# Two scatter accumulators, passes over low parts last, and merged operand splits in the experts of a decoder layer

## The reference, cut to what matters

```
scores = sigmoid(xt @ w_router)                 # 1024 tokens, 64 experts, group-limited top 8
top_w  = top_s / sum(top_s) * 2.5
# per expert e, for the tokens that chose it, in padded blocks:
hb = silu(xb @ w1[e]) * (xb @ w3[e])            # xb (block, 1024), w1 and w3 (1024, 256)
yb = hb @ w2[e]                                 # w2 (256, 1024)
routed = zeros.at[row_tok].add(yb * row_w)      # scatter-add
x = x + g2 * rmsnorm(routed + shared, norm_post_ffn)
```

## Time and profile before

| what | value |
| --- | --- |
| device time, median of 3 runs | 1926.11 us (1922.32 to 1934.88) |
| span of the profiled execution, first to last instruction | 1924.1 us |
| its device time as a whole | not recorded beside the span |
| mean granted TensorE clock | 0.957 |
| attention | about 350 to 498 us of the span |
| experts' loop, from its first to its last block | 941.4 to 1896 us |
| last stage, from the load of `acc` on | 1896.4 to 1924.1 us |

### The profile page before, as it was taken

How to read it: one execution, slowest core, us unless ns; L and a number is a source line. 1 busy time by engine, 2 the same in 40 slices (tenths; PEclk the granted TensorE clock), 3 DMA queues, 4 the chain that set the end, 5 groups by cost and what they waited for, 6 DMA issues and landing times. The chain is left out here.

```text
span 1924.1 us, 38146 instructions
## 1 busy us (share of the span) xinstructions
PE 1746.1 (91%) x10357; PEld 1353.5 (70%) x10358; DVE 1410.6 (73%) x2642; ACT 1137.8 (59%) x2188; POOL 465.8 (24%) x361
## 2 busy tenths in 40 slices
PE   3998999777599978998699999999999999999994
PEld 2787887555378756776577777777777677777773
DVE  6587651588478756666488888888888788888887
ACT  4411221477466543343477777777777677777776
POOL 0011100000022201336233333332333223333231
PEclk8999999999699978999799999999999999999997
DMA  9267610300200162428789978899888999899975
GB/s 358 82 197 208 199 53 28 130 16 17 93 6 8 33 232 77 111 79 173 243 266 294 298 220 277 252 311 332 266 260 292 315 302 284 259 285 300 316 233 194
DMA packets 132525, 380.04 MB, mean 198 GB/s; under 512 B 27365, under 2 KB 39998, under 8 KB 130380
## 3 DMA queue, kind: packets, MB, share of 16 engines
q1 hardware_dynamic: 97276, 288.36, 43.0%
q0 software_dynamic: 35168, 90.60, 19.5%
HBM read 333.82 MB, written 82.13 MB: 216 GB/s over the span
## 5 line engine op out<-in xcount | busy, mean ns | idle before, releaser
L2470 DVE TENSOR_TENSOR w_low<-w_experts,w_high 128x1024 fp32r<-128x1024 f32 x388 | 457.1, 1219 | 91.6 <-issue 63.4
L2411 ACT CAST w_high<-w_experts 128x1024 fp32r x390 | 390.0, 1049 | 94.8 <-issue 80.4
L2393 POOL DMA_INDIRECT acc<-y_rows,scatter_idx x96 | 185.0, 1927 | 604.8 <-DMA acc<-y_rows,scatter_idx 363.6
L2546 PE MATMUL rbank<-w_high,xT_high 128*128 128x512 f32 x776 | 314.7, 406 | 8.5 <-DVE xT_low L2485 8.5
L2546 PE MATMUL rbank<-w_high,xT_low 128*128 128x512 f32 x776 | 308.4, 397 | 0.0
L2546 PE MATMUL rbank<-w_low,xT_high 128*128 128x512 f32 x776 | 305.6, 394 | 0.0
L2568 PE MATMUL rbank<-w_experts,upper 128*128 x384 | 180.8, 593 | 1.9 <-DVE actT_low L2476 1.9
L2546 PEld LDWEIGHTS rbank<-w_high,xT_high 128*128 128x128 f32 x776 | 147.6, 190 | 40.2 <-DVE xT_low L2485 8.1
L2546 PEld LDWEIGHTS rbank<-w_high,xT_low 128*128 128x128 f32 x776 | 146.8, 189 | 33.4
L2546 PEld LDWEIGHTS rbank<-w_low,xT_high 128*128 128x128 f32 x776 | 147.4, 190 | 31.0
L2377 POOL DMA_INDIRECT gathered<-h,idx x96 | 137.5, 1432 | 44.5 <-issue 27.1
(11 more groups left out here) (445 smaller groups left out, 3611.7 us busy)
## 6 DMA issues: line engine op xcount, KB each, us to landing
w_experts<-in_exp_w SPq DMA_DIRECT2D x384, 512.0 KB
qT<-in_w_ada POOLq DMA_DIRECT2D x16, 1024.0 KB, 6.0
w_raw<-in_w_in SPq DMA_DIRECT2D x24, 512.0 KB, 6.8
w_ada<-in_w_ada SPq DMA_DIRECT2D x16, 512.0 KB, 15.1
p_mixed<-mixed SPq DMA_DIRECT2D x8, 512.0 KB, 8.4
w_out<-in_w_out SPq DMA_DIRECT2D x1, 4096.0 KB, 12.5
x_kept<-x SPq DMA_DIRECT2D x8, 512.0 KB
acc_tile<-acc SPq DMA_DIRECT2D x8, 512.0 KB, 7.1
```

What stands on the lines that cost most here:

```text
L2393: pool.indirect_dma_start(dr["acc"], bass.IndirectOffsetOnAxis(ap=sidx[j][:], axis=0), y[j % 2][:], None, bounds_check=S - 1, oob_is_err=F ...
L2411: act.copy(w13_s[par][0][:, which, k], w13[:, bass.ds(w, 1), which, k].squeeze(1)).then_inc(w_high, 1)
L2470: dve.tensor_tensor(w13_s[par][1][:, which, k], w13[:, bass.ds(w, 1), which, k].squeeze(1), w13_s[par][0][:, which, k], ALU.subtract).then ...
L2546: q = pe.matmul(ps_h[:].rearrange("p (a n) -> p a n", a=2), xT[a][:, k, :], w13_s[par][z][:, :, k, :], start=(k == 0 and m == 0), stop=(k ...
```

## The change

- `attend`: VectorE clears a tile of 128x1024 first of all, and SyncE writes it eight times to `acc1`, a second accumulator in HBM (4 MB), between the eight loads and the stores of `o`.
- `experts`: blocks with an even number scatter to `acc`, those with an odd number to `acc1`, each with a semaphore of its own, so that a scatter waits for the one two before it. In the end both are loaded, and VectorE adds them tile by tile.
- The copy of block `b`'s result out of PSUM moves on ScalarE from the end of turn `b` into turn `b + 1`, behind the high part of `w2`.
- Pairs of instructions become one: the two copies of `y_rows`, the two high parts and two low parts of the transposed rows, the pairs of weight splits (2048 elements instead of two times 1024; 1024 instead of two times 512 for `w2`), and the two index columns (one tile of two columns; the scatter reads its first, the gather its second).
- The copy of the gate weight (`slot_w`) moves from VectorE to ScalarE.
- TensorE does the passes over low parts last: in `up` all eight slices high-high, then all with the low part of the weights, then all with the low part of the rows, with a wait ahead of each pass; in `down` the native half first, then high-high and low-high, then the pass with the low part of `w2`.
- VectorE's turn begins with the low part of `w1` of block `b + 2`, ahead of its wait for the transposes of block `b`.

```diff
@@ attend
+            sp.wait_ge(zero_done, 1)
+            for t in range(NT):
+                sp.dma_start(dr["acc1"][t * P:(t + 1) * P, :], zero[:]).then_inc(zero_out, 16)
             for i, (h, n) in enumerate(ITEMS):
                 sp.wait_ge(o_ready, i + 1)
...
+            dve.memset(zero[:], 0.0).then_inc(zero_done, 1)
@@ experts, sync
-        sp.wait_ge(y_out, n_blocks(sp) * 16)
+        nb = n_blocks(sp)
+        sp.wait_ge(y_out[1], nb // 2 * 16)
         for t in range(NT):
-            sp.dma_start(acc_tile[t][:], dr["acc"][t * P:(t + 1) * P, :]).then_inc(acc_in[t], 16)
+            sp.dma_start(acc_tile[t][:], dr["acc1"][t * P:(t + 1) * P, :]).then_inc(acc_in[t], 16)
+        sp.wait_ge(y_out[0], (nb + 1) // 2 * 16)
+        sp.sem_inc(f_held, 1)
+        sp.wait_ge(w_high, (nb + 3) // 4 * 16 + 10)
+        sp.sem_inc(f_held, 1)
+        sp.wait_ge(w_low, (nb + 3) // 4 * 16 + 8)
+        sp.sem_inc(f_held, 1)
+        sp.wait_ge(dn_mm, (nb + 3) // 4 * 4 + 1)
+        for t in range(NT):
+            sp.dma_start(acc1_tile[t][:], dr["acc"][t * P:(t + 1) * P, :]).then_inc(acc1_in[t], 16)
@@ experts, gpsimd
                     gather(b + 4, j)
+                    pool.wait_ge(y_out[j % 2], (i * 2 + j // 2) * 16)
+                    pool.sem_inc(y_free, 1)
                     pool.wait_ge(y_ready, b + 2)
                     pool.sem_inc(held, 1)
-                    pool.wait_ge(y_out, b * 16)
-                    pool.sem_inc(y_free, 1)
-                    pool.indirect_dma_start(dr["acc"], bass.IndirectOffsetOnAxis(ap=sidx[j][:], axis=0), y[j % 2][:], None,
-                                            bounds_check=S - 1, oob_is_err=False, compute_op=ALU.add).then_inc(y_out, 16)
+                    pool.indirect_dma_start(sums_of[j % 2], bass.IndirectOffsetOnAxis(ap=idx[j][:, 0:1], axis=0), y[j % 2][:], None,
+                                            bounds_check=S - 1, oob_is_err=False, compute_op=ALU.add).then_inc(y_out[j % 2], 16)
@@ experts, scalar (the loop's body)
                     down_operands(b)
-                    split(b + 2, j % 2, PIECES[2:])
+                    y_copy(b - 1, (j + 3) % 4)
+                    split(b + 2, j % 2, range(1, 2))
                     act.wait_ge(act_ready, b + 1)
                     silu(b + 1)
-                    x_copy(b + 2)
-                    split(b + 3, (j + 1) % 2, PIECES[:2])
-                    act.wait_ge(y_free, b + 3)
-                    act.wait_ge(dn_mm, b + 2)
-                    act.copy(y[j % 2][:, 0:BANK], ps_y[0][:])
-                    act.copy(y[j % 2][:, BANK:], ps_y[1][:]).then_inc(y_ready, 1)
+                    x_copy(b + 2, (j + 2) % 4)
+                    split(b + 3, (j + 1) % 2, range(1))
@@ experts, vector (the loop's body)
-                    dve.wait_ge(at_mm, b + 1)
-                    dve.wait_ge(dn_mm, b + 1)
-                    dve.tensor_copy(aT[:], ps_a[0][:, 0:P])
...
-                    split_rest(b + 2, j % 2, (0, 1))
+                    split_rest(b + 2, j % 2, range(1))
+                    act_rest(b)
+                    indices(i, j)
                     down_rest(b)
-                    split_rest(b + 2, j % 2, (2, 3))
+                    split_rest(b + 2, j % 2, range(1, 2))
                     activate(b + 1, (j + 1) % 4)
-                    x_rest(b + 2, (j + 2) % 4)
+                    x_rest(b + 2)
...
         def times_post(t):
             dve.wait_ge(acc_in[t], 16)
+            dve.wait_ge(acc1_in[t], 16)
+            dve.tensor_tensor(acc_tile[t][:], acc_tile[t][:], acc1_tile[t][:], ALU.add).then_inc(f_added, 1)
+            dve.wait_ge(f_added, t + 1)
             dve.tensor_tensor(acc_post[t][:], acc_tile[t][:], post[:], ALU.mult).then_inc(posted, 1)
@@ experts, tensor
         def up(n, par):
+            pe.wait_ge(x_copied, n + 1)
+            pe.wait_ge(w_high, n * 4 + 4)
+            up_pass(n, par, 0, 0)
             pe.wait_ge(w_low, n * 4 + 4)
+            up_pass(n, par, 0, 1)
             pe.wait_ge(x_low, n + 1)
+            up_pass(n, par, 1, 0).then_inc(up_mm, 1)
+
+        def up_pass(n, par, a, z):
             for k in range(KC):
-                for m, (a, z) in enumerate(PASSES):
-                    q = pe.matmul(ps_h[:].rearrange("p (a n) -> p a n", a=2), xT[a][:, k, :], w13_s[par][z][:, :, k, :],
-                                  start=(k == 0 and m == 0), stop=(k == KC - 1 and m == 2))
-            q.then_inc(up_mm, 1)
+                q = pe.matmul(ps_h.rearrange("p (a n) -> p a n", a=2), xT[a][:, k, :], w13_s[par][z][:, :, k, :],
+                              start=(k + a + z == 0), stop=(k == KC - 1 and a == 1))
+            return q
```

185 lines of the change are left out of this document (100 added, 85 removed).

## The result

The changed kernel takes 1951.73 us (median of 4 runs, 1944.02 to 1953.09), beside 1926.34 us (1922.32 to 1934.88) for the kernel before: a ratio of 1.0125 [1.0098, 1.0153]. It is slower, by more than was forecast. The profiled execution has a span of 1949.4 us and a device time of 1951.17, so 1.8 us lie around the span.

The account below looks back on a forecast made before the run. It took a nearly full TensorE to bound the experts' loop; attention +9.5, the end +11 and the loop -13.9 made +6.6 us on a 1924.1 us span, 1930.7, or 1932.7 as a median, with an 80% range of 1918 to 1948.

Parts of the forecast that it names:

- the three terms of the sum: Attention's clearing +9.5, the end +11 and the experts' loop -13.9, together +6.6 us on a span of 1924.1.
- Clearing, +9.5: In attention, the first store of `o` queues behind 4 MB of zeros and holds VectorE: +9.5 us, bounds 0 and 15.
- The scatter chain stands beside a TensorE that is full, so its 363.6 us are priced at 0: In the experts' loop, GpSimd's waits for its own scatters delay nobody, so removing them gains 0.
- the 11.7 us: Time the loop holds above TensorE's floor in the 94 blocks after the first; 6 us of it were expected back.
- Pass order, -5.3: In `up`, eight slices of one tile in a row give both buffers the better one's time: -5.3 us, bounds 0 and 18.7.
- Late waits, -6 and -2.6: Waits ahead of the passes of `up` save 6 us in the loop (bounds 3 and 11.7), 2.6 at its start.
- The loop's sum: Experts' loop: -6 and -2.6 from waits and -5.3 from pass order, -13.9 us together.
- The end, +11: Last stage: eight adds on VectorE, a wait on its own result and a later start, +11 us (bounds 9.5 and 13.5).
- the term of the shift: At the end, the last scatter goes out later and shares DMA with 4 MB, delaying the start 1.5 us (0 to 3.5).
- The base: The profiled span of 1924.1 us, with the median of the runs taken to lie 2.0 us above it.
- The late activation: Rival in the loop: VectorE's activation product is pushed past its 1.8 us of slack, 1962 us; chance 9%.
- Late weights: Rival in the loop: two scatters in flight starve weights, three more experts stall, +12 us, 1945; chance 8%.

Follow-up runs that it names:

- h0: f2 with GpSimd granting the buffer of `y` ahead of its gather: 1934.71 us, ratio 1.0039 to the kernel before.
- h1: h0 with each scatter also waiting for ScalarE's high part of the rows of its turn: 1942.31 us, ratio 1.0068 to the kernel before.
- f0: The kernel before, run again unchanged: 1929.43 us, ratio 1.0021 to itself.
- e3: The kernel before with only the two accumulators, their clearing ahead of the stores and the final sum: 1944.38 us, ratio 1.0089.
- f3: The changed kernel with `up` as before, both low parts awaited first and products slice by slice: 1954.75 us, ratio 1.0152 to the kernel before.
- g2: The changed kernel with zeros spread, accumulators loaded in pairs after the last landing, odd tiles' adds on GpSimd: 1934.57 us, ratio 1.0022 to the kernel before.
- f2: The kernel before with the two accumulators and the writes of zeros spread between the stores of `o`: 1935.92 us, ratio 1.0058.
- g0: The changed kernel, run again without an edit: 1948.08 us, ratio 1.0097 to the kernel before.

## Why the prediction was wrong

It said 1932.7 with a range to 1948; it is 1951.7. On the span that is 18.7 us more than forecast. By the two profiles 9.3 of them lie in the three terms of the sum (1.8 in attention, 4.3 in the loop, 3.2 at the end) and 9.3 in pieces that the forecast left as they were. Taken by its own terms:

- **Clearing, +9.5: right in mechanism and place.** The first store landed near 386 (385 was forecast), VectorE was idle for 10.57 us. SyncE's time for issuing the writes, 3.6 us ahead of the store, was not in the account; it doesn't show in the sum, as the landing comes when the bytes ahead are through. Six profiles with the eight writes in a row have a stage of 157.2 to 160.8 us, those without 146.5 to 148.6: about 12 us, at the upper bound of the forecast's own range. The stall makes 9.5 of it (10.57 us where 1.02 stood before), just as forecast; the rest goes with the lower clock that TensorE is granted, but that this is its cause was not tried and is not clear: without the stall, h0 and h1 have 30.6 and 34.2 us at the lower level and stages of 148.2 and 148.3 us, while f0 has 27.0 and 148.6.
- **"The scatter chain stands beside a TensorE that is full, so its 363.6 us are priced at 0": the step that failed in the loop.** The reason given was that nobody waits for GpSimd. That holds, but the chain decides when gathers are issued, and behind some of them the register loads of ScalarE and VectorE last 1.0 to 1.7 us instead of 0.3, which accounts for about half of what the chain costs. This step made the forecast too pessimistic by itself, and the two below it too optimistic by more. From block 1 on, the loops with one accumulator take 930.5 to 935.6 us (950.8 with the moved copy), those with two 923.6 to 927.6 unless the gather is put in the wrong place (941.5). Of the 11.7 us that the forecast found in 94 blocks some 7 lay in eleven slightly longer blocks, which are what went in the changed kernel.
- **Pass order, -5.3: wrong.** The steps did not change when the tiles no longer alternate. The rows showed that blocks of one parity are slower, and I took alternation for the reason; parity also means another buffer of the split weights, which the change left alone. The bound of 0 was the measured end.
- **Late waits, -6 and -2.6: mis-sized.** They were booked with the 4.7 us of waits for the low part, but the second accumulator takes these away already (e3: two are left, 1.4 us). The first block went from 14.2 (11.3 in the second run of before) to 10.1; in the rest of the loop the waits give 1 to 2 us (925.0 and 926.0 beside f3's 927.3). The loop's sum was -13.9 and is -9.6: right sign, near size, and mostly for another reason than the one given; that the size came out near is luck.
- **The end, +11: the term of the shift was mis-sized, 4.6 us where 1.5 was taken.** Eight adds cost 28.8 - 19.3 = 9.5 us, as forecast. The start shifted more: the last scatter beside 4 MB of loads took 11.2 us until the loads behind it, not 6.9 (7.6 in g2, with no loads ahead), and it went out 5.1 us after the last block's start, 3.4 before. So the loads start 6.0 us later after the last block's start. VectorE begins 4.0 us behind them and not 5.3, which leaves a shift of 4.6, where 3.5 was the bound. The moved copy makes more of it than the 0.5 us that it was given: e3 and f2, without it, have ends of 49.5 and 49.3 us, 11.4 over the kernel before and near the forecast's 11.
- **The base.** The profile before was 7 us short in one piece, against its second profile, and 4.6 us long in another. The forecast took the median to lie 2.0 us above this span; 1.8 us of that is just what stands around every span, so it left no room for a profile at the short end.

The three terms make +11.3 - 9.6 + 14.2 = 15.9 us by the two profiles, where +6.6 was forecast. The second profiles of both kernels, f0 and g0, give +12.2 - 6.6 + 14.3 = 19.9, which is all of the difference between these two spans, 20.1. The medians give 25.4, and 18.6 in the repetition; what both intervals hold is 1.0098 to 1.0129, some 19 to 25 us. So the three terms can be all there is, and the sum of 15.9 is on the short side. Of what may lie between, 1 us may be routing: from the first list to block 0 the six profiles with the stall in attention take 190.0 us on the mean, the ten later ones without it 188.8, with a spread of some us in both. Whether anything more is left stays open.

None of the rivals took over. The late activation did not come: TensorE waits for it twice, 1.7 us. Late weights did not become more frequent: the loop of the changed kernel has one long block (13.9 us, block 57), as the one before has.

## What to carry to other kernels

A large transfer with no hurry, issued ahead of small stores on the same queue, costs its own duration as soon as a double buffer waits for the first of those stores: put it behind them in pieces. Before a wait of a side engine is priced at nothing, ask what else that engine issues, and where in the others' turns it falls when the wait goes or comes: here a scatter and a gather put some 4.5 us later in the block were worth 16. And a second accumulator is paid twice outside the loop, for its clearing and for its sum, which here cost 12 and 14 us against 7 gained.

## What the runs showed of the hardware

- **Register loads are slow behind a gather.** Reading one number from SBUF into a register takes 0.3 us. It takes 1.0 to 1.7 us in a fifth to a quarter of the cases where it begins 0.3 to 2.0 us after GpSimd was given a gather, and in no other place of the loop in 17 profiles. In the example above the loads of ScalarE, VectorE and SyncE are held and end within 0.7 us of each other. The page shows it only as idle time ended by "issue".
- **Stores queue behind writes that were issued first.** 64 KB took 7.1 us behind 4 MB of loads and 13.0 us with 4 MB of writes between, and SyncE was busy for 6.3 us with issuing these eight writes. The Trainium skill (DMA: Bandwidth & Descriptors, "Queues, rings and completion order") has it that every DMA engine consumes the descriptors of one ring in ring order; the trace agrees, and with the writes spread out the store is on time.
- **An adding scatter of 512 KB lands later beside loads**: from its issue to what waits for its landing 6.9 us in the kernel before and 7.6 in g2, 11.2 with eight loads of 512 KB going out around it.
- **GpSimd and VectorE slow each other.** Additions of 128x1024 float32 elements from SBUF take 1.21 us on VectorE alone and 3.25 us beside one on GpSimd, which itself takes 2.3 with VectorE idle and 2.8 to 3.4 beside it. The Trainium skill (GPSIMD Engine Reference, "1. Specifications") says that GpSimd shares its SBUF interfaces with VectorE and contends with instructions that have two SBUF inputs; the trace agrees. In all three cases of g2 VectorE's instruction ends 1.1 us after GpSimd's, which reads like waiting for it rather than sharing; nothing was tried on it.
- **Up products of the two parities differ, whatever the order.** They take 5.84 and 5.73 us in both orders, all through the loop. The parities read different buffers of split weights; that this makes the difference was not tried.
- **TensorE's granted clock falls in an idle time and stays low behind it.** In the changed kernel it was at the lower level for about 6 of 10 us without work in attention and for 4 us behind them. All six profiles with the stall have such a stretch, of 10.2 or 13.7 us, and none of the others has one in that place.
